# Two more places in SBUF for expert weights: one tile of its own, one laid over `xT` and `y`

## What is computed

```python
def layer(x):
    x = layer_norm(ALPHA * x + mixer(x))
    return layer_norm(ALPHA * x + moe(x))

def moe(x):                       # 32 experts, 2 for each of 256 tokens
    gate, expert = router(x)      # sigmoid scores, best group, top 2 in it
    for e in range(32):
        h = silu(x_e @ w1[e]) * (x_e @ w3[e])   # w1, w3: 1024 x 512
        y_e = h @ w2[e]                         # w2: 512 x 1024
    return sum of gate * y_e for each token
```

## Time and profile before

| what | value |
|---|---|
| time of three runs | 1430.96 us median (1430.59 to 1434.89) |
| time of the profiled execution | 1432.51 us |
| span of the profiled execution, first to last instruction | 1430.6 us |
| TensorE busy (PE) | 1161.7 us, 81% |
| VectorE busy (DVE) | 399.6 us, 28% |
| ScalarE busy (ACT) | 224.4 us, 16% |
| moved by DMA | 461.20 MB, mean 322 GB/s |
| mean granted TensorE clock | 0.945 of full speed |

### The profile page before, as it was taken

The page is one execution under the profiler, slowest core; times in us unless marked ns, Lnnn a source line. Parts: engine busy times, 40 slices in busy tenths (PEclk is TensorE's granted clock), DMA queues, the critical chain, the costliest instruction groups (busy, mean ns, idle before and its releaser), DMA issues. The chain is left out here.

```text
span 1430.6 us, 34064 instructions
## 1 busy us (share of the span) xinstructions
PE 1161.7 (81%) x14947; PEld 732.3 (51%) x14947; DVE 399.6 (28%) x1126; ACT 224.4 (16%) x589; POOL 14.4 (1%) x28
## 2 busy tenths in 40 slices
PE   8898779877777776759999899988987776777774
PEld 4444355544444444438778458445554444445442
DVE  1344512211111111133348744143211111111113
ACT  0123111100000010114433114110110010000001
POOL 0000100000000000010000000000000000000000
PEclk9999899989999999989999999998999999999998
DMA  9631599999999999973133341749999999999995
GB/s 361 253 118 59 211 412 425 429 423 429 424 427 427 426 427 424 427 302 118 59 118 118 118 146 62 281 198 379 424 429 425 425 426 426 427 426 428 425 424 209
DMA packets 63139, 461.20 MB, mean 322 GB/s; under 512 B 3824, under 2 KB 4000, under 8 KB 30320
## 3 DMA queue, kind: packets, MB, share of 16 engines
q1 hardware_dynamic: 61680, 455.92, 77.7%
q0 software_dynamic: 1408, 4.56, 0.8%
HBM read 459.41 MB, written 1.05 MB: 322 GB/s over the span
## 5 line engine op out<-in xcount | busy, mean ns | idle before, releaser
L803 PE MATMUL bank<-ring,arena 128*32 128x128 f32 x5568 | 191.4, 292 | 121.7 <-DMA ring<-in_moe_w 101.5
L803 PEld LDWEIGHTS bank<-ring,arena 128*32 128x32 f32 x5568 | 167.2, 114 | 142.7 <-DMA ring<-in_moe_w 82.5
L803 PE MATMUL bank<-arena 128*32 128x128 f32 x2624 | 103.2, 318 | 74.7 <-DMA arena<-in_moe_w 66.1
L1130 ACT ACTIVATE arena<-bank 128x256 f32<-128x256 f32 (+5 forms) x200 | 84.8, 431 | 368.6 <-PE bank L766 145.2
L1624 DVE SCALAR_TENSOR_TENSOR gated<-gated,bank 128x128 f32<-128x128 f32 x64 | 18.5, 288 | 428.4 <-ACT gated L1204 428.4
L763 PE MATMUL bank<-x,arena 128*32 128x256 f32 x1024 | 130.0, 637 | 4.5 <-DVEq L1585 4.5
L803 PEld LDWEIGHTS bank<-arena 128*32 128x32 f32 x2624 | 88.6, 125 | 85.8 <-DMA arena<-in_moe_w 79.3
L901 PE MATMUL bank<-xT,ring 128*128 128x256 f32 x512 | 115.2, 382 | 0.0
L901 PEld LDWEIGHTS bank<-xT,ring 128*128 128x128 f32 x512 | 96.6, 192 | 13.0 <-issue 0.4
L1204 ACT ACTIVATE gated<-bank 128x128 f32<-128x128 f32 x64 | 17.8, 278 | 466.7 <-PE bank L803 466.7
L784 PE MATMUL bank<-arena 32*128 32x256 f32 x1056 | 86.5, 444 | 4.8 <-issue 3.6
(11 more groups left out here) (229 smaller groups left out, 990.6 us busy)
## 6 DMA issues: line engine op xcount, KB each, us to landing
ring<-in_moe_w SPq DMA_DIRECT2D x131, 2048.0 KB, 40.5
arena<-in_moe_w SPq DMA_DIRECT2D x61, 2048.0 KB, 40.0
ring<-in_gdn_w_in SPq DMA_DIRECT2D x12, 2048.0 KB, 8.8
ring<-in_ab_w_in SPq DMA_DIRECT2D x5, 2048.0 KB, 23.1
ring<-in_gdn_w_out SPq DMA_DIRECT2D x4, 2048.0 KB, 8.6
ring<-in_ab_w_out SPq DMA_DIRECT2D x2, 2048.0 KB, 19.6
ring<-in_ab_w_in SPq DMA_DIRECT2D x2, 1024.0 KB, 8.2
x<-in_x SPq DMA_DIRECT2D x2, 512.0 KB, 4.4
```

The lines of the kernel that those rows point to most:

```text
L803: last = mm(psum[5][h * CAP:(h + 1) * CAP, m * FH:(m + 1) * FH], xeT[:, j], slot_tile(slots[m])[:, j, h // 2 * SEQ + h % 2:(h // 2 + 1) * ...
L1130: return do(o, i, ACT.Copy, **kw)
```

## The change

`xT` and `y` become the two halves of one tile `xy` of 16 KB per partition, which serves as slot 10; a new tile `held` is slot 9. Unit 93 (w1 of expert 31) always goes to `held`, unit 90 (w1 of expert 30) to `xy`. In layer 0 unit 93 is issued right behind the input projections, in layer 1 behind the fourth GDN unit; unit 90 is issued before unit 9 in both layers, once the router's logits and the layer norm before them are done. At the end of the layer the two are not loaded again. The SBUF for `held` comes from small tiles that move over tables no longer in use (`gates`, `cw`, `cw_in`, `wba`) and from `dynamic_dma_scratch_size`, now given as 4096.

In layer 0 the slots are dealt out anew. Attention's `pT` moves out of `arena` into `y`'s half of `xy`, so that slot 8 is free from the start: unit 4 goes there and is issued behind unit 93. Unit 5 goes to slot 7 and waits for `o_ps` (the last attention head's values) in place of `mix_ps`.

```diff
-MOE_SLOTS = ((0, 1, 2, 3, 4, 5, 6, 7, 8), (4, 5, 0, 1, 6, 2, 3, 7, 8))
+MOE_SLOTS = ((0, 1, 2, 3, 8, 7, 4, 5, 6), (4, 5, 0, 1, 6, 2, 3, 7, 8))
+HELD = {93: SLOTS, 90: SLOTS + 1}

 def slot_moe(layer, u):
-    return MOE_SLOTS[layer][u % SLOTS]
+    return HELD[u] if u in HELD else MOE_SLOTS[layer][u % SLOTS]
...
-        xT = sb("xT", [P, DJ, SEQ])
-        y = sb("y", [P, NT, D])
+        xy = sb("xy", [P, 2 * NT * D])
+        xT = xy[:, 0:NT * D].rearrange("p (j t) -> p j t", j=DJ)
+        y = xy[:, NT * D:].rearrange("p (t d) -> p t d", t=NT)
+        held = sb("held", [P, DJ, HALF])
...
-        pT = area(56, [2, 384])
+        pT = xy[:, NT * D:NT * D + 768].rearrange("p (e q) -> p e q", e=2)
...
+        spare += [held[:], xy[:].rearrange("p (j n) -> p j n", j=DJ)]
...
-        gates = sb("gates", [P, 384])
+        gates = k("mask_b")
...
+            def load_unit(layer, u):
+
+                slot = slot_moe(layer, u)
+                sp.dma_start(part(u % 3, slot), expert_parts(layer, u // 3)[u % 3]).then_inc(slot_full[slot], 16)
...
-                for n in range(DEPTH):
-                    load_expert(n, n, lambda m: first_free(3 * n + m))
-                for n in range(DEPTH, GROUP):
-                    load_expert(n, n, freed(n))
+                for u in range(SLOTS):
+                    if u not in early:
+                        first_free(u)
+                        load_unit(layer, u)
+                sp.wait_ge(lgT_ps, NT * (layer + 1))
+                sp.wait_ge(x_ready, 4 * layer + 2)
+                load_unit(layer, 90)
                 with sp.Fori(1, NE // GROUP) as i:
                     for c in range(GROUP):
                         load_expert(i * GROUP + c, c, freed(i * GROUP + c))
-                for n in range(NE // GROUP * GROUP, NE):
-                    load_expert(n, n % GROUP, freed(n))
+                for u in range(NE // GROUP * GROUP * 3, 3 * NE):
+                    if u not in HELD:
+                        freed(u // 3)(u % 3)
+                        load_unit(layer, u)
...
+            early = (4,)
+            load_unit(0, 93)
+            load_unit(0, 4)
             for h in range(2):
                 sp.wait_ge(proj_ps, 2 * h + 2)
                 load_att(6 + h, tiles(a["ab_w_out"][0], slice(h * HALF, (h + 1) * HALF)))
...
             def free_for_moe0(u):
                 if u < 4:
                     sp.wait_ge(proj_ps, 2 * (u + 2) + 2)
+                elif u == 5:
+                    sp.wait_ge(o_ps, HEADS)
                 else:
                     sp.wait_ge(mix_ps, 4)
...
+                if u == 3:
+                    sp.wait_ge(fast[0].w1_used, NE)
+                    load_unit(1, 93)
...
-    nc = bacc.Bacc("TRN2", target_bir_lowering=False, num_devices=1)
+    nc = bacc.Bacc("TRN2", target_bir_lowering=False, num_devices=1, dynamic_dma_scratch_size=4096)
```

More of the change, by code:

```diff
@@ L335, in build @@
         g_norm = gates_of([1])
-        cw = sb("cw", [P, P])
-        cw_in = sb("cw_in", [P, P])[:]
-        wba = sb("wba", [P, DJ, 32])
+        cw = k("mask_a")[:, 0:P]
+        wba = k("mask_a")[:, P:3 * P].rearrange("p (j n) -> p j n", j=DJ)
+        cw_in = const[:, COLS["cos"][0]:COLS["cos"][0] + P]
         flag = sb("flag", [P, 2, 2], I32)
@@ L343, in build @@
             sem(n) for n in ("ident_in", "const_in", "small_in", "ln_in", "gdn_in", "out_done"))
-        slot_full = [sem(f"slot_full{i}") for i in range(SLOTS)]
+        slot_full = [sem(f"slot_full{i}") for i in range(SLOTS + len(HELD))]
         x_half = [sem(f"x_half{t}") for t in range(NT)]
@@ L439, in load_gdn, with load_experts @@
                 sp.dma_start(ring[:, slot_gdn(u)], src).then_inc(slot_full[slot_gdn(u)], 16)
-            def load_experts(layer, first_free):
+            def load_unit(layer, u):
+                slot = slot_moe(layer, u)
+                sp.dma_start(part(u % 3, slot), expert_parts(layer, u // 3)[u % 3]).then_inc(slot_full[slot], 16)
+            def load_experts(layer, first_free, early=()):
                 s = fast[layer]
@@ L508, in free_for_moe0 @@
                     sp.wait_ge(proj_ps, 2 * (u + 2) + 2)
+                elif u == 5:
+                    sp.wait_ge(o_ps, HEADS)
                 else:
                     sp.wait_ge(mix_ps, 4)
-            load_experts(0, free_for_moe0)
+            load_experts(0, free_for_moe0, early)
             load_more(0)
@@ L793, in turn @@
                         ends_here = ends and c == cs[-1]
-                        slots = [slot_of(3 * c + m) for m in range(3)]
+                        slots = [slot_of(3 * (n if ends else c) + m) for m in range(3)]
                         filled = [full(i, c, m) for m in range(3)]
@@ L834, in full @@
                 def full(i, c, m):
-                    slot = slot_moe(layer, 3 * c + m)
+                    u = 3 * c + m
+                    if isinstance(i, int):
+                        u += 3 * i * GROUP
+                    slot = slot_moe(layer, u)
+                    if u in HELD:
+                        return slot_full[slot], 16 * (MOE_BASE[layer][slot] + 1)
                     return slot_full[slot], i * 16 + 16 * (MOE_BASE[layer][slot] + 1)
@@ L848, in moe @@
                         mm(psum[h][:], ident, y[:, :, h * Q:(h + 1) * Q], start=True, stop=False)
-                    experts(more[layer], NIT - NE, lambda u: u, more_ready)
+                    experts(more[layer], NIT - NE, lambda u: u % SLOTS, more_ready)
                 with pe.Else():
@@ L1218, in gdn @@
                 act.wait_ge(cw_ps, 1)
-                copy(cw[:], psum[7][:, 0:P]).then_inc(cw_sb, 1)
+                copy(cw, psum[7][:, 0:P]).then_inc(cw_sb, 1)
                 evacuate_xT(2)
```

6 lines of the change are left out of this document (3 added, 3 removed).

## The result

The changed kernel takes 1414.4 us (median, 1413.0 to 1416.33) against 1432.93 us for the kernel before (1430.59 to 1436.74) in the same comparison: a ratio of 0.987, 95% interval 0.9847 to 0.9893, which is 15.3 to 21.9 us. A second comparison on another occasion gave 0.9856 (0.9835 to 0.9876). The profiled execution took 1413.0 us with a span of 1411.2.

What follows compares the result with a forecast made beforehand. Weight loads bound the two expert stages. Layer 0 gains 12.1 - 1.5 - 0.75 = 9.85 us, layer 1 6.0 - 1.5 - 0.75 = 3.75, together 13.6; 1430.96 - 13.6 = 1417.4, say 1417, range 1410 to 1423.

Steps and rivals of the forecast that it cites:

- A unit that is moved out of a plateau into a hole is worth 4.92 us: Both expert stages: each weight load moved to idle DMA time saves 4.92 us, as long as PE can follow.
- The gap is 0 to 1.3 us. I take 1.0.: Layer 0, DMA queue ahead of unit 9: it runs dry for 0 to 1.3 us, taken as 1.0.
- get 13.8 us for the stream's end: Layer 0: three units fewer, 14.76 us, less the 1.0 us gap, end the weight stream 13.8 us sooner.
- PE is the later one, and the gain is ... 12.1 us: Layer 0, w2 of expert 31: PE's steps reach it at 609.0, the stream would allow 607.4; gain 12.1 us.
- 2.8 of its 4.92 us fall in that hole, and unit 9 and everything after it is 2.1 us later: Layer 1: unit 90 fills the empty queue ahead of unit 9 for 2.8 us and delays the later stream by 2.1.
- 7.2 + 2.8 + 10.4 + 1.95 + 4.06 = 26.4: Layer 1: PE's steps from w3 of expert 29 to w2 of expert 31 take 26.4 us, ending at 1406.2; gain 6.0.
- I take 1.5, nearer to nothing: End of each layer: written-out experts 30 and 31 stall as new code, bounds 0 and 4.9 us, 1.5 taken.
- I take half of it in each layer: End of each layer: a slow-clock dip costs PE 1.5 us once it is the later one; half is charged, 0.75.
- the stream stays the limit: Rival, both layers: no code stall or clock dip; gain at most 14.8 + 7.7 = 22.5 us, time 1409 to 1414; chance 0.15.
- the holes: Sign, DMA rate ahead of unit 9: no hole longer than 1.3 us in layer 0 and none in layer 1.
- the releases of w1: Sign, end of both layers: w1 of experts 30 and 31 is released by ACT and not by a DMA.
- the missing waits at w3: Sign, end of both layers: w3 (and w2) of experts 30 and 31 start with no DMA idle.

Runs made afterwards that it cites:

- four off: The change with w1 of experts 28 and 29 also not loaded, their matmuls reading the two held places (wrong results): 1396.64 us, 0.9756 to the kernel before.
- no early units: The change with units 4 and 5 of layer 0 issued behind the attention output as before, 93 and 90 still held: 1421.27 us, 0.9917 to the kernel before.
- short end: The change with half of the w1 and w3 matmuls of experts 30 and 31 left out, loads the same: 1413.28 us, 0.985 to the kernel before.
- second trace: Another trace of the same kernel, no edit: the change 1414.01 us, 0.9856 to the kernel before; the kernel before 1434.16 us against 1434.97.
- Layout alone: The change's tiles, tables, slots and descriptor scratch only, no unit held and none early: 1432.6 us, 0.9994 to the kernel before.
- early units only: The change with units 4 and 5 of layer 0 early but no unit held, 90 and 93 loaded at the end: 1428.48 us, 0.9963 to the kernel before.

## Why the prediction was right, and where it was off

**Right in mechanism and sign.** 1417 was forecast within 1410 to 1423; 1414.4 was measured. "A unit that is moved out of a plateau into a hole is worth 4.92 us" held with the hole counted: 4.2 to 4.6 us for the second held unit in layer 1, 4.0 to 4.3 us a unit with four off. In layer 0 with one unit held it is less exact, see below.

**The gain was taken too small.** The sum was 13.6 us and the measured difference 18.5, with 15.3 as its lower end. That is outside the band of 10 to 17 us to which the forecast gave 0.60. The forecast time came out closer, 3 us off, only because the kernel before stood 2 us higher in this comparison; that part is luck. By steps:

- *"The gap is 0 to 1.3 us. I take 1.0."* One microsecond at 66 GB/s: right. Layer 1: no hole left, as forecast.
- *"get 13.8 us for the stream's end"*, layer 0: unit 95 landed 12.9 us sooner, as the mean of two traces.
- *"PE is the later one, and the gain is ... 12.1 us"*, layer 0: 12.4 as the mean of two traces. In the first, w1 of expert 31 stands 10.3 us behind that of expert 30 (10.44 forecast), and w2 3.79 us behind w3 (4.06). PE is the later one in both, by 1.1 and 0.3 us where the sum had 1.6: right in sign.
- *"2.8 of its 4.92 us fall in that hole, and unit 9 and everything after it is 2.1 us later"*, layer 1: w3 of expert 29 starts on its weight 425.17 and 425.02 us after the start of the stage, against 424.57 and 424.32 in the kernel before. That is 0.6 to 0.7 us later, not 2.1; three more versions that load unit 90 there (90 held alone, no early units, short end) have 425.1 to 425.9. So the hole was worth 4.3 us of the 4.92 in the change's traces, and 3.5 to 4.3 in the others. The sum counted it from the last bytes to the first ones, but the earlier trace rows has slices on both sides in which the rate is far from full: 283 and 23 GB/s before, 113, 249 and 181 behind. Mis-sized by 1.4 us. It put the stream's end 7.7 us sooner, and the landings have 9.0.
- *"7.2 + 2.8 + 10.4 + 1.95 + 4.06 = 26.4"*, layer 1: measured 1393.07 - 1368.22 = 24.85 in the first trace and 1393.84 - 1367.38 = 26.46 in the second. The 7.2 has a slow group in it, as the trace before has the earlier trace rows. The second trace has one too (3.14 us, then w2 after 7.19 us), and so has layer 0 in both traces; the first trace of layer 1 has none, and there the step is 1373.90 - 1368.22 = 5.7. So the term was right three times in four.
- *"I take 1.5, nearer to nothing"* for code new to the sequencer, in each layer: nothing of the kind stands in the first trace's ends, 0.34 us in the second's. The written-out experts don't stall as the first pass does. Mis-sized by 3 us.
- *"I take half of it in each layer"* for the slow clock: this counts the slow group a second time, since the 7.2 already has it. Behind it nothing waits for a weight for long, and the clock is full. In the first trace the last 36 us of layer 1's experts ran at a granted clock of 1.00, the top level of 2.4 GHz, with PE busy for 30.43 of them, where the kernel before has 0.91 over 39 us with 29.57 busy and idle gaps of 2.7 us. Windows of both, in the columns of the earlier trace rows, first the changed kernel, then the kernel before:

```profile
1360.00:1396.00 36.00, 30.43 (x619) 19.75 (x619) 6.50 (x21) 5.25 (x13) 0.00 (x0) 1.00 0.87 366
```

```profile
1377.00:1416.00 39.00, 29.57 (x523) 19.03 (x523) 4.75 (x15) 4.49 (x11) 0.00 (x0) 0.91 0.85 359
```

  In the second trace the slow group stands in a window (1366 to 1374) at 0.79, and the steps behind it (1374 to 1393) are at 1.00. Mis-sized by 1.5 us. The rule that the Trainium skill (TensorE: Matmul & The Clock Gate, Part 1) gives, that activity lifts the slow clock, agrees with both traces; I had cited it and not used it. A wait of 2.6 to 2.8 us doesn't always bring the slow clock: in layer 1 of the two traces the group behind it took 2.05 us once and 3.14 us once.

Without the three mis-sized terms (1.5 twice, 0.75 twice, 1.4 for the hole) the same sum gives 19.5 us, inside the measured interval. The rival "the stream stays the limit", to which I gave 0.15, comes closest to what was found: its bounds of 14.8 and 7.7 us, 22.5 together, against 12.4 and 8.2. It isn't quite that, since PE is later than the stream in three of the four ends.

**Of the signs I gave,** the holes, the releases of w1 and the missing waits at w3 came as forecast. w2 of expert 31 in layer 0 starts at 607.67 where I had 611. Counted from unit 9's issue, w2 of layer 1 comes 7.3 us sooner in the first traces and 5.2 in the second ones, where I had 3.75. One sign of being wrong showed in part: w2 of expert 31 waits for its weight in layer 1 of the first trace, by 0.52 us. The other two did not: "issue" idles are 0 and 0.34 us in an end, and no full slice is below 420 GB/s.

**Costed at nothing, and so it was:** the delayed output projections, the GDN's loads, the moved tables and the smaller descriptor scratch. Layout alone, which has the last two, gave 0.9994; for the first two the table of stages shows no cost.

**What isn't settled.** With unit 90 alone held the count gives layer 0 two units less than before, 9.8 us, and the trace has 8.0; with 93 alone three less the hole, 9.6 to 9.9, and the trace has 8.8. Traces of one kernel differ by 0.4 to 1.9 us in this stage, so I don't read more into it. What sets the granted clock that the first expert of layer 1 gets, 1.00 in five of the twelve traces and 0.64 to 0.67 in the others, isn't known, and neither is why the stretch between the layers differs by 2 us and more.

Of the versions that compute everything none is faster than the change; the one with the w1 of experts 27 and 28 held is its equal.

## What to carry to other kernels

Where a stage is bound by a stream of loads, count the units between the moment when the queue last runs full and the end, and ask of each edit how many it takes away and what the queue does ahead of the first slot that must be freed: two measures that move units forward can each be worth one and together nearly three (4.5, 4.9 and 12.4 us here), because a hole swallows the difference. Size a hole by all the bytes that it lacks, the slices in which the rate falls and rises included, and not by its empty slices alone. Find idle bandwidth and dead tiles by stage, since a tile that is needed only between stages is a slot during one.

When pricing the consumer's steps, decide where a disturbance (a slow group, a stall of new code) is counted: in the base step or as a term of its own. Here it stood in both. And before reading 2 us into one stage of one trace, look at a second trace of the same kernel. Where the question is whether the consumer or the stream ends a stage, the landing of the last load answers it directly; the releaser alone doesn't say by how much.

## What the hardware showed that I had not expected

A DMA queue that has run dry comes back in two steps: with early units only, unit 9 is issued at 181.48, its bytes flow from 182, the rate drops to 66 to 98 GB/s for a microsecond and is at 360 and more from 184. The same dip stands in the changed kernel at 183, without an empty slice before it. Unit 10 was issued at 183.21 in the one and 183.56 in the other, when w3 of expert 0 had been used, and the rate comes back 0.4 to 0.8 us later. That this is the cause of the dip is likely; it wasn't tried.

In the first pass through the expert code PE has idle times with no wait behind them, 2.15 and 2.75 us in the earlier trace rows, and 1.08 to 2.49 us in the two traces of the change. In the written-out experts at the end, where no wait for weights hides them either, there are next to none (0.34 us once).
